# Where three column groups of a modulation vector are computed: first feed-forward or recurrence

## What is computed

```python
sh1_l, sc1_l, g1_l, sh2_l, sc2_l, g2_l = jnp.split(jax.nn.silu(c) @ ada_w[i] + ada_b[i], 6, axis=-1)
hl = modulate(rms_norm(xl, norm_mix[i]), sh1_l, sc1_l)
...
xl = xl + g1_l[:, None] * yl
hl2 = modulate(rms_norm(xl, norm_ffn[i]), sh2_l, sc2_l)
xl = xl + g2_l[:, None] * expert_choice_ffn(hl2, router[i], w_gate[i], w_up[i], w_down[i])
```

```python
def advance(s, u_c, wk_c, kd_c, cd_c):
    w = u_c - jnp.einsum('bhck,bhkv->bhcv', wk_c, s)
    return w, cd_c * s + jnp.einsum('bhck,bhcv->bhkv', kd_c, w)
```

## Time and profile before

| | us |
|---|---|
| median of 3 runs | 2806.91 (2806.54 to 2809.15) |
| the profiled execution, its own time | 2808.67 |
| its span | 2806.9 |
| TensorE busy (matmuls) | 2728.1 (97%) |
| VectorE busy | 1136.7 (40%) |
| ScalarE busy | 520.7 (19%) |
| GpSimd busy | 536.2 (19%) |

### The profile page before, as it was taken

One profiled execution on the slowest core, in us unless ns is written; L12 is line 12 of the kernel. 1 busy time (PEld: TensorE's weight loads), 2 busy tenths in 40 slices (PEclk: granted clock), 3 DMA queues, 4 the chain that ended last, 5 costly groups with the idle time before them and its releaser, 6 DMA issues. The chain is left out here.

```text
span 2806.9 us, 36231 instructions
## 1 busy us (share of the span) xinstructions
PE 2728.1 (97%) x15236; PEld 1781.5 (63%) x15236; DVE 1136.7 (40%) x2213; ACT 520.7 (19%) x1156; POOL 536.2 (19%) x371
## 2 busy tenths in 40 slices
PE   8999999999999999999999999999989999998998
PEld 5444467777886445888888745788733338873333
DVE  2325533444412233444433175666232235652223
ACT  1424420000001133110000231434110010011011
POOL 1000003233342010244443110011010004431000
PEclk9999999999999999999999999999999999999999
DMA  8211025775222211222221400210399972238994
GB/s 266 92 44 57 30 90 211 270 269 205 84 84 100 90 72 45 91 78 88 72 83 41 175 29 20 82 33 10 126 368 421 421 315 75 92 118 357 420 421 200
DMA packets 70042, 431.21 MB, mean 154 GB/s; under 512 B 8202, under 2 KB 9017, under 8 KB 25720
## 3 DMA queue, kind: packets, MB, share of 16 engines
q1 hardware_dynamic: 65080, 412.56, 38.5%
q0 software_dynamic: 4800, 16.33, 1.7%
HBM read 422.41 MB, written 13.79 MB: 155 GB/s over the span
## 5 line engine op out<-in xcount | busy, mean ns | idle before, releaser
L467 PE MATMUL bank<-h,weight_ring 128*128 128x256 f32 x912 | 218.8, 383 | 1.1 <-DVE arena L391 1.0
L467 PEld LDWEIGHTS bank<-h,weight_ring 128*128 128x128 f32 x912 | 170.6, 190 | 36.8 <-issue 13.3
L1287 PE MATMUL bank<-h,weight_ring 128*128 128x512 f32 (+2 forms) x464 | 179.8, 539 | 0.6 <-DVE h L273 0.6
L3407 PE MATMUL bank<-h,weight_slots 128*128 128x256 f32 (+1 forms) x576 | 173.4, 457 | 7.1 <-DVE weight_slots L3434 6.3
L622 PE MATMUL bank<-arena,weight_ring 128*128 128x256 f32 x704 | 155.0, 379 | 0.0
L3407 PEld LDWEIGHTS bank<-h,weight_slots 128*128 128x128 f32 x576 | 108.4, 191 | 68.9 <-issue 48.2
L622 PEld LDWEIGHTS bank<-arena,weight_ring 128*128 128x128 f32 x704 | 133.7, 190 | 18.5 <-issue 0.4
L2862 PE MATMUL bank<-weight_slots,tokens_T 128*64 128x512 f32 x592 | 143.1, 598 | 2.1 <-issue 2.1
L467 PE MATMUL bank<-h,arena 128*128 128x256 f32 x608 | 143.6, 379 | 0.0
L1287 PEld LDWEIGHTS bank<-h,weight_ring 128*128 128x128 f32 (+1 forms) x464 | 84.8, 188 | 89.3 <-issue 86.0
L467 PEld LDWEIGHTS bank<-h,arena 128*128 128x128 f32 x608 | 115.6, 190 | 15.7
(11 more groups left out here) (556 smaller groups left out, 4494.5 us busy)
## 6 DMA issues: line engine op xcount, KB each, us to landing
arena<-in_ada_w SPq DMA_DIRECT2D x48, 1024.0 KB, 4.9
weight_ring<-in_gu SPq DMA_DIRECT2D x44, 1024.0 KB, 5.0
weight_slots<-in_w_up SPq DMA_DIRECT2D x42, 1024.0 KB, 26.0
weight_slots<-in_w_down SPq DMA_DIRECT2D x34, 1024.0 KB, 21.7
weight_slots<-in_w_gate SPq DMA_DIRECT2D x32, 1024.0 KB, 22.6
weight_ring<-in_w_gate SPq DMA_DIRECT2D x32, 1024.0 KB, 23.2
weight_ring<-in_w_down SPq DMA_DIRECT2D x30, 1024.0 KB, 24.0
weight_ring<-in_down SPq DMA_DIRECT2D x32, 704.0 KB, 4.2
```

What stands on the lines that cost most here:

```text
L467: m = pe.matmul(self.bank(q, i), weights[:, c * P:(c + 1) * P], tokens[:, c, :], start=(c == 0), stop=(c == 3))
L1287: m = pe.matmul(out, lhs, rhs, start=(c == 0), stop=(c == last - 1))
L3407: m = pe.matmul(self.bank(n)[:, 0:hi - lo], slot.buf[:, at:at + P], self.h[:, c, lo:hi], start=(c == 0), stop=(c == KT - 1))
```

## The change

The last three of the twelve groups, which are the second half of the second layer's modulation (shift, scale and gate of its feed-forward), are no longer computed by `Modulation` but by a new class, `LateModulation`, inside the recurrence. `Modulation` keeps 9 groups and so 36 parts.

A late part covers all 8 slices of the contraction for 64 columns in each of four strips: 32 matmuls of 64 columns instead of 8 of 256, from a panel of the same size. Four panels fit: they use the space of the output weights, which are now fetched last. The parts take the place of the fillers: parts 0 to 2 in step 0 (where smaller fillers stay around `chunk_ends`), one part at the first place of each step from 1 to 5, two parts at the second place of steps 1 and 2. VectorE copies a whole 128x256 bank for each group (`keep`, in steps 1, 3 and 5), TensorE turns the rows in step 5 with 6 matmuls of 128x128 by 4 columns (`turn`), and VectorE adds them to the bias in one instruction (`add`).

```diff
-    STRIPS, STRIP, WIDTH, GROUPS, PARTS = 4, 32, 256, 12, 4
+    STRIPS, STRIP, WIDTH, GROUPS, PARTS, LAYER = 4, 32, 256, 9, 4, 24
...
+class LateModulation:
...
+    FIRST, GROUPS, DEPTH = 9, 3, 4
...
+    def fetch(self, sp, n, weights):
+        if n >= self.DEPTH:
+            after(sp, self.done, n - self.DEPTH)
+        sp.dma_start(self.panels[n % self.DEPTH], weights[n]).then_inc(self.landed[n % self.DEPTH].sem, 16)
+
+    def part(self, pe, n):
+        g, i = divmod(n, Modulation.PARTS)
+        if g >= 2 and i == 0:
+            after(pe, self.kept, g - 2)
+        after(pe, self.landed[n % self.DEPTH], n // self.DEPTH)
+        w = Modulation.WIDTH // Modulation.PARTS
+        for t in range(KT):
+            for s in range(Modulation.STRIPS):
+                at, panel = s * STRIP, (t * Modulation.STRIPS + s) * w
+                m = pe.matmul(self.bank(g)[at:at + 2, i * w:(i + 1) * w], self.cond[:, t, :], self.panels[n % self.DEPTH][:, panel:panel + w],
+                              start=(t == 0), stop=(t == KT - 1))
+        m.then_inc(self.done.sem, 1)
+
+    def keep(self, v, g):
+        after(v, self.done, (g + 1) * Modulation.PARTS - 1)
+        v.tensor_copy(self.rows[:, g, :], self.bank(g)).then_inc(self.kept.sem, 1)
...
+    def turn(self, pe):
+        after(pe, self.kept, self.GROUPS - 1)
+        out = self.turned_cols().rearrange("p (g s j) -> p g s j", g=self.GROUPS, j=2)
+        for g in range(self.GROUPS):
+            for j in range(2):
+                m = pe.matmul(out[:, g, :, j], self.rows[:, g, j * P:(j + 1) * P], self.k.ident[:, 0:P:STRIP], start=True, stop=True)
+        m.then_inc(self.turned.sem, 1)
+
+    def add(self, v):
+        after(v, self.turned, 0)
+        v.tensor_tensor(self.cols, self.turned_cols(), self.cols, ALU.add).then_inc(self.added.sem, 1)
...
-                gated0.slots[FT - 1].fetch(sp, a["gu0"][FT - 1])
+                for t in range(17, FT):
+                    gated0.slots[t].fetch(sp, a["gu0"][t])
...
+        PARTS_AT = {(0, 0): (0, 1, 2), (1, 0): (3,), (1, 1): (4, 5), (2, 0): (6,), (2, 1): (7, 8), (3, 0): (9,), (4, 0): (10,), (5, 0): (11,)}
...
-                for i in range(4):
-                    out.fetch(sp, i, a["ev2_out"])
+                for n in range(4):
+                    late.fetch(sp, n, a["ada_late"])
                 c.store_growth(sp)
                 for j in range(LAT_FROM, STEPS):
                     c.fetch_gates(sp, j)
                     c.fetch_growth(sp, j)
+                    for n in {2: (4, 5, 6, 7, 8, 9), 3: (10, 11)}.get(j, ()):
+                        late.fetch(sp, n, a["ada_late"])
+                for i in range(4):
+                    after(sp, late.done, late.parts - late.DEPTH + i)
+                    out.fetch(sp, i, a["ev2_out"])
...
                     if j:
-                        stay_busy(k, pe, 3, 1, HALF)
+                        late_parts(j, 0)
                         c.use_state(pe, j - 1, 0)
...
                         gates.seen(pe, "gam_col")
+                        stay_busy(k, pe, 1, 1, HALF)
                         c.chunk_ends(pe)
-                        stay_busy(k, pe, 1, 3)
+                        stay_busy(k, pe, 3, 1, HALF)
+                        late_parts(0, 0)
                         for d in range(2):
                             c.level_z(pe, j, d, 0)
...
-                    if 0 < j <= LAT_FROM:
-                        stay_busy(k, pe, 3, 3, HALF)
+                    if j:
+                        late_parts(j, 1)
...
                         c.level_update(pe, j, 1, n)
+                        if n == 2 and j == LAST:
+                            late.turn(pe)
...
                         c.level_y(v, j, 0, n)
+                        if n == 1 and j in (1, LAST):
+                            late.keep(v, 0 if j == 1 else 2)
+                        if n == 3 and j == LAST:
+                            late.add(v)
                         c.level_mask(v, j, 1, n)
...
                         c.level_y(v, j, 1, n)
+                        if n == 1 and j == 3:
+                            late.keep(v, 1)
```

22 lines of the change are left out of this document (20 added, 2 removed).

## The result

The kernel with the change takes 2814.7 us, median of 14 runs (2811.1 to 2818.4); the kernel before, run on the same chip in turn with it, takes 2808.2 us (14 runs, 2806.0 to 2813.6). The ratio is 1.0022, with a 95% interval of 1.0015 to 1.0030: about 6 us **slower**. I had forecast 2801.1 us, with a range of 2798 to 2808 us. The sign was wrong and the time lies outside the range. The profiled execution of after took 2815.05 us, its span is 2813.2 us; before it was 2808.67 and 2806.9 us.

A forecast was written before the change was run, and what follows sets the result against it. The matmul engine was taken to bound the kernel, busy 2728.1 of 2806.9 us; feed-forward -14.5, step 0 +3.3 and +1.2, places +1.0 and +0.65, keep, turn and add +2.4 gave -5.9, so 2801.1 us, range 2798 to 2808.

The forecast's parts named there:

- The feed-forward: First feed-forward: removing 12 parts at 1.173 us each and 24 of 96 little matmuls saves 14.5 us.
- What one part costs: A late part in the recurrence, 64 traced matmuls in four strips, takes 1.1 us, bounds 1.05 to 2.2 us.
- Rival (a): Late parts pay per instruction: 2.2 us each at 34 ns, so 2812 us; 2806 at 25 ns; chance 0.12.
- Step 0: Recurrence's first step: waiting for panels of parts 0 to 2 costs 3.3 us, half clock into the levels 1.2 us.
- the test: Forecast is wrong if the recurrence's first step loses under 2 or over 7 us, or a part takes over 1.3 us.
- First places: Steps 1 to 5, before `use_state`: one part replaces a filler, 0.2 us later each, +1.0 us in all.
- Second places: Steps 1 and 2: two parts of 2.15 us replace filler and wait, +0.4 and +0.25, together +0.65 us.
- Keep, turn, add: Recurrence: bank copies +0.9 us, turning the rows in step 5 +1.4, the addition +0.1, together +2.4 us.
- Queues: Gates, growth rows and output weights queued behind panels on SP still arrive in time, so they cost nothing.
- Rival (b): Half clock returns in steps 1 and 2 too, up to 1.7 us per dip: 2804.5 us; chance 0.15.
- Rival (d): A panel or gate row lands late because loads share engines, stalls of several us: 2810 us; chance 0.06.

The follow-up runs named there:

- experiment 1: Kernel before with 9 groups in `Modulation`, groups 9 to 11 left out altogether and the recurrence untouched: 2794.27 us, ratio 0.9954.
- experiment 3: Kernel before with its fillers in the places replaced by streams of small matmuls like a part's, without any panel or load: 2809.76 us, ratio 1.0005.
- experiments 6 and 7: Each 1 MB load issued as four of 256 KB: in the changed kernel with fillers for parts, 2805.40 us; in the changed kernel itself, 2822.94 us.
- extra_load: Kernel before with one more 1 MB output-weight load behind the growth rows of each of steps 3, 4 and 5, no parts: 2810.33 us, ratio 1.0007.
- one_group: Changed kernel with only group 11 late, four parts in steps 1 to 4, output weights loaded one by one, three behind growth rows: 2809.88 us, ratio 1.0009.
- two_paced: Changed kernel with two late groups, eight parts in steps 1 to 5, loads issued one or two at a time at step starts: 2807.60 us, ratio 0.9994.

## Why the prediction was wrong, point by point

- **The feed-forward, -14.5:** right. -14.3 in the traces, -14.1 by experiment 1.
- **What one part costs, 1.1 us (bounds 1.05 to 2.2):** right, 1.07 us. Rival (a), a price per instruction, is dead: 64 matmuls in 1.07 us are 16.7 ns each. The floor of 25 ns that the Trainium skill gives (TensorE: Matmul & The Clock Gate, section "Wait — 56ns, not 53.3ns?"), which I had weighed in rival (a), does not hold for four strips of columns side by side either.
- **Step 0, +3.3 and +1.2:** right in kind, 1.9 us too small. The third panel took 10.3 us and not 9.1, and there were 10.2 us of half clock, from 1741.5 and from 1748.3 us, where I had reckoned with one stretch of 3.4. 5.25 us to the first level and 1.12 behind it. It stays inside the 2 to 7 us that I had set as the test.
- **First places, 5 x 0.2:** too much, 5 x 0.1. The other column of my own row, the 0.21 us of waiting, went as I said. **Second places, 0.65:** too much, 0.1. I had taken two parts as 2 x 1.07, but from the first part's start to the next instruction it is 1.90 us for 128 matmuls, since the groups overlap at their ends.
- **Keep, turn, add, 2.4:** right, 2.1. The keep of step 3 is hidden.
- **Queues, "I cost these at nothing":** here it failed. The sentence was about gates, growth rows and output weights, and of those it holds: none came late, and no engine waits for one at a step's start. What I left out is that a load is not only a thing with a due time. It also keeps the DMA engines busy when a packet of TensorE's program is due, and the packets in front of the three stops started about 4 us late. In the same way I costed a part only by its duration in the place of a filler, and not by its 128 instructions against the filler's 4. The two together made 7.6 us of stops and 3.0 us behind them at half clock: 10.6 of the 12 us by which I was off. The other 1.9 are step 0's, and the over-estimates of places and keeps pay for the 0.8 of slow supply in step 4.
- **Rival (b), half clock in more steps:** it happened, in steps 1 and 2, and with about the price that I gave (up to 1.7 us each), but not for the reason named. It followed stops. In experiment 3, where the same thin matmuls run in the same places without a stop, the granted clock over the whole recurrence (1745 to 1965 us) is 0.99 (after: 0.97).

```profile
1745.00:1965.00 220.00, 206.95 (x4806) 183.38 (x4806) 141.12 (x315) 91.37 (x295) 22.48 (x16) 0.99 0.12 41
```

```profile
1745.00:1965.00 220.00, 197.19 (x4822) 181.69 (x4824) 132.13 (x302) 85.77 (x284) 22.50 (x16) 0.97 0.25 87
```

- **Rival (d), something lands late:** its kind was right (the parts' own loads share the engines with others) and so was its sign; the victim was another, and the time of 2810 us was short by 5. I gave it 0.06. A chance of 0.08 for slower was too little for a change that adds eight loads and nine parts (576 matmuls) to the most tightly fed part of the kernel.

The prediction rested on five more rows of before that do not stand in its groups: the fillers of steps 3 and 5, the narrow additions, the fourth output weight, and the stretch that is shown above.

```profile
721.56 0.48 DVE L1032 TENSOR_TENSOR vectors<-bank,vectors 128x24 f32<-128x24 f32 x4
...
1753.36 0.68 SPq L3637 DMA_DIRECT2D gate_rows<-in_ev_out  x1
...
1851.13 0.70 PE L114 MATMUL bank<-constants 128*128 128x256 f32 x2
...
1922.99 0.70 PE L114 MATMUL bank<-constants 128*128 128x256 f32 x2
```

**What stays open.** Which property of a load delays a packet (long rows are not needed for it, by experiments 6 and 7). Why the stops of `extra_load` are together only a third of those of `one_group`; the packets' boundaries also fall on other instructions there, and I did not tell the two apart. Why the clock fell at some stops and not at longer ones. And a version of the late part with fewer and wider matmuls, which would use up less program in the same time, was not tried.

## What to carry to other kernels

A stretch of very short matmuls lives on its supply of program: before moving work into it, count its instructions and its loads, and not only its microseconds. A filler that looks like waste may be the time in which the next packet arrives, and a load that has tens of us to spare may still cost time by when it goes out. The sign to look for is a wait for "issue" inside a group of equal matmuls, with packets of the instruction queue far apart in front of it and the last of them 2 to 3 us before its end. And the half of a change that works may be worth keeping alone: one group of three, its loads spread, gives 4.5 us, where all three lose 6.

## What the runs showed of the hardware

- TensorE's program comes in packets of 16384 bytes, one for each 256 matmuls and weight loads. In the levels' streams of 64-column matmuls 256 instructions last some 4 us, in the parts half of that. A packet's first instruction began 2.15 us after the packet's start at the earliest. Each of 37 stops, of 0.4 to 3.9 us, stood on the first instruction of a packet that had started with 108 or fewer instructions left; with more left there was none.
- With 1 MB loads under way, a packet started up to 4.6 us (`two_paced`) after TensorE had begun the last 256 instructions that it held; in before, in steps 1 to 5, at most 0.9 us.
- Four matmuls of 64 columns in four strips of 2 output rows run side by side: 64 matmuls in 1.07 us, 16.7 ns each, in the time in which 32 in pairs of strips go by the earlier trace rows.
- A stop of 1.8 us was followed by half clock for 3.4 us; one of 1.9 us elsewhere in the same kernel was not. Over all runs the three stops above 2.6 us were, those of 2.27 and 2.19 us were not.
- Loads of 1 MB cut into four issues were no faster in either try: 2.8 us slower, not clear of the noise, and 8 us slower.
